# A second pair of feed-forward steps by seven block products, with the weight sums made by adding transfers

## The reference, cut to what matters

```
x = x + 0.5 * (silu(h @ w_gate) * (h @ w_up)) @ w_down      # h = rmsnorm(x), w_gate and w_up 1024x2816, w_down 2816x1024
x = x + mixer(x)
x = x + 0.5 * swiglu(rmsnorm(x), second set of weights)
```

## Time and profile before

| | |
|---|---|
| median of 3 runs | 1147.89 us (1147.51 to 1148.63) |
| profiled execution | 1147.37 us, its span 1145.6 us |
| PE busy | 1137.4 us (99%), 5477 matmuls |
| DVE busy | 927.9 us (81%) |
| ACT busy | 615.3 us (54%) |
| POOL busy | 211.7 us (18%) |
| moved by DMA | 235.82 MB, mean 206 GB/s |

### The profile page before, as it was taken

The page is one execution under the profiler, slowest core; times in us unless marked ns, Lnnn a source line. Parts: engine busy times, 40 slices in busy tenths (PEclk is TensorE's granted clock), DMA queues, the critical chain, the costliest instruction groups (busy, mean ns, idle before and its releaser), DMA issues.

```text
span 1145.6 us, 15668 instructions
## 1 busy us (share of the span) xinstructions
PE 1137.4 (99%) x5477; PEld 932.3 (81%) x5477; DVE 927.9 (81%) x1434; ACT 615.3 (54%) x789; POOL 211.7 (18%) x413
## 2 busy tenths in 40 slices
PE   9999999999999999999999999999999999999997
PEld 7888888888777888888888888888877788888886
DVE  6878886878987687789788788867898695988895
ACT  6455645457764454455454555454677635454453
POOL 2221230062000012121301221302510000122221
PEclk9999999999999999999999999999999999999999
DMA  8976575795325578756659756647953435886552
GB/s 296 312 265 209 165 232 167 239 263 193 125 75 184 184 233 268 260 164 223 205 194 298 256 175 224 207 154 216 274 164 108 141 136 183 284 283 217 162 196 103
DMA packets 168080, 235.82 MB, mean 206 GB/s; under 512 B 17376, under 2 KB 112848, under 8 KB 168016
## 3 DMA queue, kind: packets, MB, share of 16 engines
q1 hardware_dynamic: 146720, 222.23, 59.0%
q0 software_dynamic: 11008, 8.80, 3.2%
q10 hardware_dynamic: 10288, 4.00, 1.4%
HBM read 221.86 MB, written 1.05 MB: 195 GB/s over the span
## 4 chain that ended last, share of the span: by engine, by line
PE 99%; DVE 1%; issue 0%; ACT 0%; POOLq 0%; POOL 0%; DVEq 0%
PE ps L1645 28%; PE ps L1647 28%; PE ps L1646 28%; PE ps L1778 2%; PE ps L1779 2%; PE ps L1777 2%; PE ps L1903 2%; PE ps L1959 2%; PE ps L1931 2%; PE ps L1695 1%; PE ps L1664 1%; DVE wlo L639 0%; PE ps L1874 0%; PE ps L2082 0%; PE ps L1990 0%; PE ps L1950 0%
## 5 line engine op out<-in xcount | busy, mean ns | idle before, releaser
L639 DVE TENSOR_TENSOR wlo<-raw,whi 128x2048 fp32r<-128x2048 f32 (+2 forms) x195 | 427.5, 2198 | 80.5 <-ACT whi L1347 54.0
L1347 ACT ACTIVATE whi<-raw 128x2048 fp32r<-128x2048 f32 (+2 forms) x195 | 359.2, 1843 | 206.4 <-PE ps L1647 160.2
L1645 PE MATMUL ps<-whi,ht_hi 128*128 128x512 f32 (+1 forms) x1064 | 415.8, 391 | 0.6 <-DVE wlo L639 0.6
L1647 PE MATMUL ps<-whi,ht_lo 128*128 128x512 f32 (+1 forms) x1064 | 411.0, 386 | 0.0
L1646 PE MATMUL ps<-wlo,ht_hi 128*128 128x512 f32 (+1 forms) x1064 | 410.5, 386 | 0.0
L1645 PEld LDWEIGHTS ps<-whi,ht_hi 128*128 128x128 f32 x1064 | 199.9, 188 | 40.9 <-ACT whi L1347 1.0
L1647 PEld LDWEIGHTS ps<-whi,ht_lo 128*128 128x128 f32 x1064 | 199.8, 188 | 40.9
L1646 PEld LDWEIGHTS ps<-wlo,ht_hi 128*128 128x128 f32 x1064 | 200.1, 188 | 38.6
L536 POOL DMA_DIRECT2D act_blocks<-act_blocks x224 | 110.0, 499 | 458.0 <-DVE act_blocks L709 458.0
L1645 PE MATMUL ps<-whi,at_hi 128*128 128x512 f32 x304 | 118.5, 390 | 0.0
L1646 PE MATMUL ps<-wlo,at_hi 128*128 128x512 f32 x304 | 118.3, 389 | 0.0
(11 more groups left out here) (235 smaller groups left out, 1266.9 us busy)
## 6 DMA issues: line engine op xcount, KB each, us to landing
raw<-in_ffn_w_down_dram SPq DMA_DIRECT2D x88, 512.0 KB, 4.4
raw<-in_w_in_dram SPq DMA_DIRECT2D x88, 512.0 KB, 4.6
raw<-in_ffn_w_gate_dram SPq DMA_DIRECT2D x77, 512.0 KB, 4.0
raw<-in_ffn_w_up_dram SPq DMA_DIRECT2D x77, 512.0 KB, 5.0
T_raw<-in_ffn_w_gate_dram SPq DMA_DIRECT2D x16, 512.0 KB, 5.8
T_raw<-in_ffn_w_up_dram SPq DMA_DIRECT2D x16, 512.0 KB, 5.9
raw<-in_w_out_dram SPq DMA_DIRECT2D x16, 512.0 KB, 4.3
raw<-in_ffn_w_gate_dram SPq DMA_DIRECT2D x19, 256.0 KB, 2.9
```

The lines of the kernel that those rows point to most:

```text
L639: nc.vector.tensor_tensor(wlo[:, n, 0:w], raw[:, n, 0:w], whi[:, n, 0:w].bitcast(F32), ALU.subtract).then_inc(lo_done, 1)
L1347: nc.scalar.activation(whi[:, n, 0:w], raw[:, n, 0:w], ACT.Copy).then_inc(hi_done, 1)
L1645: nc.tensor.matmul(o, xh, wh, start=start, stop=False)
L1647: return nc.tensor.matmul(o, xl, wh, start=False, stop=stop)
```

## The change

- **A second pair.** `PAIRED` gives the parts (0, 1), (1, 0) and (1, 1) a pair at step 4 besides that at 8; the part (0, 0) keeps one. The order of a part is a list, `ffn_plan`: behind a pair comes an ordinary gate/up step and then the down products that have been waiting, so 0, 1, 2, 3, (4, 5), 6, 7, (8, 9), 10, with down products 3, 4, 5 behind gate 6 and 7, 8, 9 behind gate 10.
- **Sums by transfers.** DVE's `block_sum` is gone. SP loads one block (w_gate for T1, w_up for T3); ACT makes its negative in place (`sum_start`); a transfer issued by POOL adds another block from HBM to it (`add_part`, `accum_op=ALU.add`). T2 starts as a copy of T3, T4 as the negative of T2. Per pair that is two loads of 1 MB, four copies on ACT and four adding transfers of 1 MB, in place of four loads and four subtractions on DVE.
- **Two through the ring.** T2 and T4 are no longer split ahead; they take slabs of the ring (`convert_sum` on ACT and DVE), though SP loads nothing for them. T1 and T3 stay outside.
- **Order.** For a first pair, loads of T1 and T3 stand behind the two slabs of gate 1, and the sums are made in steps 0 to 3. For the second pair of a part they stand behind the two slabs of gate 6 (`parts`), ahead of down 3, and `sum_start` comes at three places of ACT's order: inside and behind the first pair, and behind step 6. POOL issues its adding transfers ahead of `cross_act` of a step. Side sums and their rests stay in steps 1 to 3.
- **Two buffers for turned products** in place of three, changing with the parity of the step; `turn_product` waits for `act_rest` two steps before. POOL's and PE's loops over steps become straight code.

The core of the diff (in the order definitions, DVE, POOL, ACT, PE, SP):

```diff
+PAIRED = {(0, 0): (8,), (0, 1): (4, 8), (1, 0): (4, 8), (1, 1): (4, 8)}
+def ffn_steps(l, f):
+    steps, i = [], 0
+    while i < NSTEP:
+        steps.append((i, i in PAIRED[l, f]))
+        i += 2 if i in PAIRED[l, f] else 1
+    return steps
+def ffn_plan(l, f):
+    plan, waiting = [], []
+    for i, pair in ffn_steps(l, f):
+        if pair:
+            plan += [("b11", i, 0), ("b11", i, 1), ("T2", i), ("b21", i), ("b22", i), ("T4", i)]
+            waiting += [i, i + 1]
+        else:
+            plan += [("gate", i, 0), ("gate", i, 1)] + [("down", j) for j in waiting]
+            waiting = [i]
+    return plan + [("down", j) for j in waiting]
...
-        act_turns = [(v[:, 0:512], v[:, 512:1024]) for v in
-                     (act_blocks, sum_raw["T3"][:, 0:1024], sum_raw["T3"][:, 1024:2048])]
+        sg_2 = act_2 = gated_all[:, 0:1024].rearrange("p (t c) -> p t c", t=NT)
+        act_turns = [(v[:, 0:512], v[:, 512:1024]) for v in (act_blocks, gated_all[:, 1024:2048])]
...
+            def convert_sum(l, f, name, p):
+                s = SLAB_AT[l, f, name, p]
+                n = slot(l, s)
+                wait_hi(dve, l, s)
+                wait_used(dve, l, s - 3)
+                nc.vector.tensor_tensor(wlo[:, n, :], sum_raw[name][:, :], whi[:, n, :].bitcast(F32),
+                                        ALU.subtract).then_inc(lo_done, 1)
...
-            def block_sum(l, f, m):
-                r = l * 2 + f
-                b11, b12, b22, b21 = (sum_raw[n][:, :] for n in SUMS)
-                o, a, b, parts = ((b11, b12, b11, (0, 1)), (b12, b22, b12, (2,)), (b22, b22, b11, ()),
-                                  (b21, b21, b22, (3,)))[m]
-                for n in parts:
-                    dve.wait_ge(part_in[n], (r + 1) * 32)
-                if m:
-                    dve.wait_ge(sum_done, r * 4 + m)
-                nc.vector.tensor_tensor(o, a, b, ALU.subtract).then_inc(sum_done, 1)
...
+            def paired(l, f, p):
+                r, z, at = l * 2 + f, PAIR_NUMBER[l, f, p], lambda *key: SLAB_AT[(l, f) + key]
+                convert_sum(l, f, "T2", p)
+                convert(l, at("b21", p))
+                convert(l, at("b22", p))
+                dve.wait_ge(pair_out, z * 2 + 2)
+                dve.wait_ge(pair_ps, z * 2 + 2)
                 nc.vector.tensor_tensor(v57, ps[:, 0, :], m5_out, ALU.add).then_inc(pair_sum, 1)
-                dve.wait_ge(pair_ps, r * 4 + 3)
+                wait_used(dve, l, at("T2", p))
                 nc.vector.tensor_tensor(u2, ps[:, 3, :], m1_out, ALU.add).then_inc(pair_sum, 1)
-                dve.wait_ge(pair_sum, r * 5 + 2)
+                convert_sum(l, f, "T4", p)
+                dve.wait_ge(pair_sum, z * 5 + 2)
                 nc.vector.tensor_tensor(up_1, v57, u2, ALU.add).then_inc(pair_sum, 1)
-            def pair_products(l, f):
-                r, s0 = l * 2 + f, f * (FFN_SLABS + MIX_SLABS)
-                dve.wait_ge(pair_sum, r * 5 + 3)
-                wait_used(dve, l, s0 + PAIR_SLAB + 3)
+                convert(l, at("gate", p + 2, 0))
+                dve.wait_ge(pair_sum, z * 5 + 3)
+                wait_used(dve, l, at("b22", p))
                 nc.vector.tensor_tensor(up_0, ps[:, 2, :], u2, ALU.add).then_inc(pair_sum, 1)
-                dve.wait_ge(pair_sum, r * 5 + 4)
-                dve.wait_ge(silu_done, r * (2 * NSTEP) + PAIR * 2 + 2)
+                dve.wait_ge(pair_sum, z * 5 + 4)
+                dve.wait_ge(silu_done, r * (2 * NSTEP) + p * 2 + 2)
                 nc.vector.scalar_tensor_tensor(act_2[:, 0, :], up_0, rstd[:, 0:1], sg_2[:, 0, :], ALU.mult,
                                                ALU.mult).then_inc(act_done, 2)
-                dve.wait_ge(pair_ps, r * 4 + 4)
+                wait_used(dve, l, at("T4", p))
                 nc.vector.tensor_tensor(gate_1, ps[:, 0, :], u2, ALU.add).then_inc(pair_sum, 1)
-                dve.wait_ge(silu_done, r * (2 * NSTEP) + PAIR * 2 + 4)
+                convert(l, at("gate", p + 2, 1))
+                dve.wait_ge(silu_done, r * (2 * NSTEP) + p * 2 + 4)
                 nc.vector.scalar_tensor_tensor(act_2[:, 1, :], up_1, rstd[:, 1:2], sg_2[:, 1, :], ALU.mult,
                                                ALU.mult).then_inc(act_done, 2)
+                act_rest(l, f, p - 1)
+                turn_product(l, f, p)
+                turn_product(l, f, p + 1)
+                convert(l, at("down", p - 1))
+                convert(l, at("down", p))
+                products(l, f, p + 2)
+                act_rest(l, f, p)
+                turn_product(l, f, p + 2)
+                convert(l, at("down", p + 1))
+                act_rest(l, f, p + 1)
...
+            def add_part(l, f, p, m):
+                z = PAIR_NUMBER[l, f, p]
+                wg, wu = ((ffn1_w_gate, ffn1_w_up), (ffn2_w_gate, ffn2_w_up))[f]
+                w, row = ((wu, 0), (wu, 512), (wg, 0), (wg, 512))[m]
+                pool.wait_ge(part_neg[m], z + 1)
+                part = w[ds(l, 1), ds(row, 512), ds(p * FSTEP, 512)].rearrange("a (k p) c -> p (a k) c", p=P)
+                pool.dma_start(sum_raw[SUMS[m]][:, :].rearrange("p (k c) -> p k c", k=4), part, accum_op=ALU.add)\
+                    .then_inc(part_added[m], 16)
             def ffn(l, f):
                 norm(l * 3 + 2 * f)
-                with pool.Fori(1, PAIR) as i:
-                    cross_act(pool, l, f, i, BY_POOL, act_crossed_rest)
-                pool.drain()
-                for i in range(PAIR, NSTEP):
+                p0 = PAIRED[l, f][0]
+                for i in range(1, NSTEP):
+                    for m in {p0 - 3: (0, 1), p0 - 2: (2,), p0 - 1: (3,)}.get(i, ()):
+                        add_part(l, f, p0, m)
+                    for before, p in zip(PAIRED[l, f], PAIRED[l, f][1:]):
+                        for m in {before: (1,), before + 3: (0, 2, 3)}.get(i, ()):
+                            add_part(l, f, p, m)
+                    if i == PAIRED[l, f][-1]:
...
+            def sum_start(l, f, p, m):
+                z, name = PAIR_NUMBER[l, f, p], SUMS[m]
+                if m < 2:
+                    eng.wait_ge(part_in[m], (z + 1) * 32)
+                else:
+                    eng.wait_ge(part_added[m - 1], (z + 1) * 16)
+                    if z:
+                        k = [key for key, n in PAIR_NUMBER.items() if n == z - 1][0]
+                        wait_lo(eng, k[0], SLAB_AT[k[0], k[1], name, k[2]])
+                src = sum_raw[name if m < 2 else SUMS[m - 1]]
+                nc.scalar.activation(sum_raw[name][:, :], src[:, :], ACT.Copy, scale=1.0 if m == 2 else -1.0)\
+                    .then_inc(part_neg[m], 1)
...
+            def sums_behind(l, f, i):
+                p0 = PAIRED[l, f][0]
+                if i == p0 - 4:
+                    sum_start(l, f, p0, 0)
+                    sum_start(l, f, p0, 1)
+                if i == p0 - 3:
+                    sum_start(l, f, p0, 2)
+                    sum_round(l, f, p0, 0)
+                if i == p0 - 2:
+                    sum_start(l, f, p0, 3)
+                    sum_round(l, f, p0, 1)
+                if i + 2 in PAIRED[l, f][1:]:
+                    sum_start(l, f, i + 2, 3)
+                    sum_round(l, f, i + 2, 0)
+                    sum_round(l, f, i + 2, 1)
+            def paired(l, f, p):
+                z, at = PAIR_NUMBER[l, f, p], lambda *key: SLAB_AT[(l, f) + key]
+                again = next((q for q in PAIRED[l, f] if q > p), None)
+                convert_sum(l, f, 2, p)
+                convert(l, at("b21", p))
+                wait_used(eng, l, at("b11", p, 1))
+                nc.scalar.activation(m1_out, ps[:, 1, :], ACT.Copy).then_inc(pair_out, 1)
+                convert(l, at("b22", p))
+                eng.wait_ge(pair_ps, z * 2 + 1)
+                nc.scalar.activation(m5_out, ps[:, 2, :], ACT.Copy).then_inc(pair_out, 1)
+                act_round(l, f, p - 1)
+                convert_sum(l, f, 3, p)
+                convert(l, at("gate", p + 2, 0))
+                wait_used(eng, l, at("b21", p))
+                pair_silu(l, f, 0, ps[:, 1, :])
+                convert(l, at("gate", p + 2, 1))
+                convert(l, at("down", p - 1))
+                eng.wait_ge(pair_sum, z * 5 + 5)
+                pair_silu(l, f, 1, gate_1)
+                if again:
+                    sum_start(l, f, again, 1)
+                cross_act(eng, l, f, p, BY_ACT, act_crossed)
+                convert(l, at("down", p))
+                cross_act(eng, l, f, p + 1, BY_ACT, act_crossed)
+                silu(l, f, p + 2, False)
+                act_round(l, f, p)
+                convert(l, at("down", p + 1))
+                cross_act(eng, l, f, p + 2, BY_ACT, act_crossed)
+                act_round(l, f, p + 1)
+                if again:
+                    sum_start(l, f, again, 0)
+                    sum_start(l, f, again, 2)
...
```

(27 more changed lines are left out.)

463 lines of the change are left out of this document (219 added, 244 removed).

## The result

The changed kernel takes **1221.09 us**, median of 4 runs (1220.47 to 1222.39), against 1147.8 before in the same comparison: ratio **1.064, 95% interval 1.062 to 1.066**, slower. The forecast was 1163 with a range of 1142 to 1181. The sign was right, the size was not: the kernel lost 73 us where 15 were forecast.

A forecast was written before the change was run, and what follows sets the result against it. PE, busy 99%, was taken as the bound: number of matmuls times their spacing. 1147.4 - 8.2 + 17.1 + 4.5 + 2.1 = 1162.9, with 0.5 for the median 1163 us; range 1142 to 1181.

The forecast's parts named there:

- the price of the adding transfers: POOL's adds into the sums: plain 1 MB load price of 5.5 us taken in the sum, 8.3 us left to a rival.
- Rival B: Adding transfers take twice the data time, delaying the way into both pairs: 1173 to 1190 us, say 1180; chance 0.17.
- the lower clock: PE's first matmuls behind a wait may start at 1.2 GHz: taken as nothing, bound 2 us per wait.
- the first part: Part (0, 0), which keeps its one old pair, its sums having a step each: nothing counted.
- Down 3: First down slab behind the first pair lands late: PE waits 5.7 us in each of three parts, +17.1; bounds 2.5 to 7.
- The way into the first pair: Steps 1 to 3: later crossing and ACT's copies delay the slab of gate 3; +1.5 us per part, +4.5; bounds nothing to 4.
- The second pair: Rests of T1 and T3 late behind ACT's passes, with the gate edge behind the pair: +0.7 us per part, +2.1.
- Removed matmuls and their spacing: Second pairs in three parts remove 36 matmuls at 0.2267 us each, all on the path: -8.2 us.

## Why the prediction was wrong

**The failed step is the price of the adding transfers.** The forecast weighed 5.5 us to land one MB, as a plain load, against twice the data time, and put the plain price in the sum because bytes and rows are those of the T loads. The runs give 5.8 against 2.9 us of the engines' time per MB, and landings of 8.9 to 10.3 us against 5.7 to 7.3 (14.6 against 8.4 for two in a row). With plain transfers the same kernel is 36 us faster. That is half the loss, and 36 of the 58 us above the forecast. The Trainium skill ("Collectives: The Full Stack", The bandwidth ceiling) has reducing transfers at half the rate of copies, and the trace agrees to a few per cent; the same rate holds here for an add from HBM into SBUF.

**Rival B had the mechanism, and its sizes where it gave one.** It had the crossing of step 1 3 us late, and the trace has 4.5; it had the pair that follows 4 us late, and the waits at the second pair's start and its second b11 half add up to 3.9 us in part (0, 1). Its 1180 is 41 us short all the same. What it lacked is the lower clock (some 13 us), the first part (6.0), and the many waits of 2 us and less. Its chance was 0.17. The forecast had noticed that POOL issues the adds ahead of the crossing "on one queue" and put no number to it. The Trainium skill ("DMA: Bandwidth & Descriptors", Two DMAs through the same engine are not ordered) says that within one queue of a DMA engine descriptors start in order. The traces agree: with an add ahead, GpSimd's blocks took 9.5 against ScalarE's 5.8 us, and 11.6 against 6.3 in the run with late loads; with plain transfers ahead 5.3 against 5.7, and with nothing ahead 4.3 against 4.8.

**The lower clock was taken as nothing** within a bound of 2 us for each of three waits. It is some 13 us in the changed kernel and 11 with plain transfers. In the changed kernel it came up seven times in the feed-forward parts, each at a cost of 1.4 to 2.5 us: 2.4 and 2.2 behind the waits of 4.5 and 5.3 us in part (0, 1), 1.5 and 1.7 behind those of 5.4 and 5.2 us for down 3 in the other two. So the bound was nearly right for one wait; wrong were the nothing in the sum and the number of waits.

**Down 3: right, with two errors that cancel.** Forecast 5.7 us in each of three parts; measured 5.5, 5.6 and 5.3. The slab lands 11.0 us after its issue where 12 were forecast, and without the T loads ahead the wait is gone. But it was issued 16.2 us behind the pair's start and not 12.6 to 13.4, and landed at 27.2 and not 25.2; PE asked for it at 32.0 and not 29.9, so the wait came out as it should. The 10.4 us from landing to ready are 10.3 in the trace. Since down 3 gives its wait to the next slab when the loads are moved, it was however not the only thing late by then.

**The way into the first pair** (1.5 per part) was 4.1 to 4.7 us at down 1 and 0.9 us more at the pair's first sum product in part (0, 1), where PE waited for the side rests. With plain transfers it was 2.8 us in part (0, 1), 0.6 at down 1 and 2.2 at the next gate slab, which is inside the forecast's bounds.

**The second pair** (0.7) was 2.5 at its start and 1.4 at its second b11 half in part (0, 1), and neither is there with plain transfers. Both ways hang on the order of ACT's work: silus stand behind passes over sums, which stand behind crossings and adds. **The first part** (nothing) was 6.0 us, by the same order: 2.2 us on the silu's product, the rest in four waits below 1 us.

**The sum again, by the runs.** With plain transfers, as the forecast assumed, the kernel ran 1185.2: 22 above 1163, of it 11 for the clock, 3 for down 1 and the gate slab behind it (7.3 in three parts against 4.5), the rest in waits of 1.3 us and less. The adds' data time brings the other 36. Removed matmuls and their spacing were right (-8.2).

**Left open.** What the many waits of 0.4 to 1 us owe to the adds each was not taken apart. Why an added MB takes twice the engines' time is not shown by these runs, only that it does. Crossings on another queue than the adds were not tried, nor two pairs with the old sums on DVE.
